# Expert stage of a hybrid decoder step: half of one weight split on GpSimd two experts ahead, tanh ahead of y's copies, gated rows turned in pieces of 128 and 384 columns

## What is computed

```
g_sel = argmax(softmax(x @ rg_w + rg_b))              # 1 of 4 groups
top_v, top_i = top_k(e_logits of that group, 2)       # 2 of its 8 experts
def expert_block(xb, e):                              # xb: 128 rows of one expert
    return (silu(xb @ w1[e]) * (xb @ w3[e])) @ w2[e]  # 1024 -> 512 -> 1024
y = sum over a token's two experts of weight * its row
```

## Time and profile before

| | |
|---|---|
| median of 3 runs | 2290.57 us (2289.27 to 2293.32) |
| profiled execution | 2292.72 us, span 2291.2 us |
| busy: TensorE, weight loads | 95%, 78% of the span |
| busy: VectorE, ScalarE, GpSimd | 65%, 43%, 18% |
| granted TensorE clock, mean | 0.974 |

### The profile page before, as it was taken

One profiled execution on the slowest core, in us unless ns is written; L12 is line 12 of the kernel. 1 busy time (PEld: TensorE's weight loads), 2 busy tenths in 40 slices (PEclk: granted clock), 3 DMA queues, 4 the chain that ended last, 5 costly groups with the idle time before them and its releaser, 6 DMA issues. The chain is left out here.

```text
span 2291.2 us, 34192 instructions
## 1 busy us (share of the span) xinstructions
PE 2184.5 (95%) x10675; PEld 1796.3 (78%) x10676; DVE 1485.8 (65%) x2864; ACT 975.2 (43%) x1569; POOL 412.0 (18%) x564
## 2 busy tenths in 40 slices
PE   6999999999899999994889999999999999989998
PEld 5888888888688888883668887888888878857775
DVE  4787777777656666554635466686666666955564
ACT  4433333334332222221535355575555555723332
POOL 1021101110234333232100000000000000033332
PEclk9999999999899999996999999999999999999999
DMA  7111101111634433322895668697775778944431
GB/s 227 58 39 65 63 33 64 64 63 70 223 102 110 145 126 134 106 79 92 304 367 190 251 217 332 250 397 290 287 276 199 289 290 324 341 153 145 156 132 54
DMA packets 160332, 407.13 MB, mean 178 GB/s; under 512 B 18835, under 2 KB 22347, under 8 KB 160014
## 3 DMA queue, kind: packets, MB, share of 16 engines
q1 hardware_dynamic: 138518, 337.17, 41.3%
q0 software_dynamic: 14560, 43.11, 5.6%
q10 hardware_dynamic: 7200, 26.22, 2.8%
HBM read 330.12 MB, written 84.82 MB: 181 GB/s over the span
## 5 line engine op out<-in xcount | busy, mean ns | idle before, releaser
L234 PE MATMUL bank<-w_hi,mix_x 128*128 128x512 f32 x816 | 338.9, 415 | 9.8 <-DMA mix_x<-xT_dram 4.3
L236 PE MATMUL bank<-w_hi,mix_x 128*128 128x512 f32 x816 | 329.0, 403 | 0.0
L235 PE MATMUL bank<-w_lo,mix_x 128*128 128x512 f32 x816 | 328.2, 402 | 0.0
L2175 DVE TENSOR_TENSOR w_lo<-raw,w_hi 128x2048 fp32r<-128x2048 f32 x130 | 289.5, 2286 | 35.6 <-ACT w_hi L2112 34.6
L2077 PE MATMUL bank<-w_hi,x_hi 128*128 128x512 f32 x784 | 306.3, 391 | 4.3 <-DVE w_lo L2175 2.2
L2079 PE MATMUL bank<-w_hi,x_lo 128*128 128x512 f32 x784 | 306.2, 391 | 0.0
L2078 PE MATMUL bank<-w_lo,x_hi 128*128 128x512 f32 x784 | 306.0, 390 | 0.0
L2112 ACT ACTIVATE w_hi<-raw 128x2048 fp32r<-128x2048 f32 x130 | 239.0, 1932 | 5.5 <-DMA raw<-in_w 5.5
L234 PEld LDWEIGHTS bank<-w_hi,mix_x 128*128 128x128 f32 x816 | 159.8, 196 | 43.2 <-issue 5.1
L236 PEld LDWEIGHTS bank<-w_hi,mix_x 128*128 128x128 f32 x816 | 159.6, 196 | 36.0
L235 PEld LDWEIGHTS bank<-w_lo,mix_x 128*128 128x128 f32 x816 | 160.1, 196 | 31.4
(11 more groups left out here) (315 smaller groups left out, 4101.6 us busy)
## 6 DMA issues: line engine op xcount, KB each, us to landing
raw<-in_w SPq DMA_DIRECT2D x128, 1024.0 KB, 8.3
shared<-in_w SPq DMA_DIRECT2D x64, 1024.0 KB, 11.5
y_dram<-y_sb ACTq DMA_DIRECT2D x50, 512.0 KB
xT_dram<-mix_x SPq DMA_DIRECT2D x34, 512.0 KB, 3.6
mix_x<-xT_dram SPq DMA_DIRECT2D x34, 512.0 KB, 4.5
shared<-in_w_in SPq DMA_DIRECT2D x24, 512.0 KB, 6.1
small<-in_x_prompt SPq DMA_DIRECT2D x16, 512.0 KB
xr_sb<-in_x_prompt SPq DMA_DIRECT2D x16, 512.0 KB
```

The costliest lines, as they stand in the source:

```text
L234: pe.matmul(bank[:, :], x_hi[:, k, :], wh[:, k, :], start=(k == 0), stop=False)
L235: pe.matmul(bank[:, :], x_hi[:, k, :], wl[:, k, :], start=False, stop=False)
L236: ins = pe.matmul(bank[:, :], x_lo[:, k, :], wh[:, k, :], start=False, stop=(k == KD - 1))
L2175: dve.tensor_tensor(w_lo[slot(j, m)][:, cols], raw[m][:, cols], w_hi[slot(j, m)][:, cols].bitcast(F32), ALU.subtract).then_inc(lo_ready, 1)
```

## The change

GpSimd computes the second half of the low half of w1 for expert e + 2, at the end of its turn of expert e, once ScalarE has written the high half; it counts a semaphore of its own, `w1_lo`. VectorE leaves that piece out (it still makes it for experts 0 and 1, and the same half of the gate weights that follow the last expert). Whoever waited for this piece waits for `w1_lo`; the counts of `lo_ready` are re-reckoned (`wait_lo`). GpSimd's loop over experts is unrolled by four. ScalarE computes tanh ahead of `y_out`. The gated rows are made, turned and copied in pieces of 128 and 384 columns; TensorE turns half of the next rows, then the first piece, then the other half, then the second piece, and y's products go by k over both column halves.

```diff
+                def wait_lo(eng, e, m, c):
+                    if m == 0 and c == 1:
+                        eng.wait_ge(w1_lo, e + 1)
+                    else:
+                        eng.wait_ge(lo_ready, 5 * e + (1, 2 + c, 4 + c)[m])
 # SyncE, reload(e)
-                                    sp_.wait_ge(lo_ready, 2 * parts_before(e - 1, m) + c + 1)
+                                    wait_lo(sp_, e - 1, m, c)
 # GpSimd
+                        def split_w1(e, j):
+                            cols = slice(RH, 2 * RH)
+                            hold(pool, hi_ready, 2 * parts_before(e, 0) + 2)
+                            pool.tensor_tensor(w_lo[slot(j, 0)][:, cols], raw[0][:, cols], w_hi[slot(j, 0)][:, cols].bitcast(F32),
+                                               ALU.subtract).then_inc(w1_lo, 1)
                         def expert(e, j):
                             first, end = span(pool, e)
                             with pool.Fori(first, end) as i:
...
                                 load_list(...)
                                 gather(i + 1)
+                            if not isinstance(e, int) or e + 2 < NE:
+                                split_w1(e + 2, j + 2)
 # TensorE
-                            transposes(i + 1)
                             for n in range(2):
+                                transposes(i + 1, n)          # four of the eight; xe_tp after n = 1
                                 pe.wait_ge(hid_ready, 2 * i + n + 1)
-                                for k in range(2 * n, 2 * n + 2):
+                                for k in range(*K_OF[n]):     # K_OF = ((0, 1), (1, 4))
...
+                            for part, ks in enumerate(K_OF):
+                                pe.wait_ge(hidT_hi_ready, 2 * i + part + 1)
+                                for k in range(*ks):
+                                    for w in (wh, wl):
+                                        for n in range(2):
+                                            pe.matmul(Y[n][:, :], hidT_hi[:, k, :], col(w, k, n), ...)
+                            pe.wait_ge(hidT_lo_ready, 2 * i + 2)
+                            for n, done in enumerate((y0_mm, y1_mm)):
+                                for k in range(KF):
+                                    ins = pe.matmul(Y[n][:, :], hidT_lo[:, k, :], col(wh, k, n), ...)
+                                ins.then_inc(done, 1)
 # ScalarE, block_of
-                            y_out(i)
                             act.wait_ge(h1_mm, i + 1)
                             act.activation(tanh_h[:, :], H1[:, :], ACT.Tanh, scale=0.5).then_inc(tanh_done, 1)
+                            y_out(i)
 # VectorE, after
+                                theirs = part[1:] == (j + 2, 0) and not (isinstance(e, int) and e + 2 == NE)
+                                split(*part, halves=(0,) if theirs else (0, 1))
```

More of the change, by code:

```diff
@@ L1903, in program @@
             lo_ready = sem("lo_ready")
+            w1_lo = sem("w1_lo")
             late_loaded = sem("late_loaded")
@@ L1928, in program @@
                 quarter = lambda bank: bank[:, :].rearrange("p (k n) -> p k n", k=4)
-                pair_of = lambda bank: quarter(bank)[:, 0:2, :]
+                K_OF = ((0, 1), (1, KF))
+                parts_of = lambda bank, n: quarter(bank)[:, 0:K_OF[n][1] - K_OF[n][0], :]
                 (xe_tp, xe_hi_ready, xe_lo_ready, h1_mm, h3_mm, tanh_done, up_done, hid_ready,
@@ L2017, in _ @@
                             for c in range(2):
-                                sp_.wait_ge(lo_ready, 2 * parts_before(NE - 1, n) + c + 1)
+                                wait_lo(sp_, NE - 1, n, c)
                                 sp_.dma_start(raw[n][:, c * RH:(c + 1) * RH].rearrange("p (k n) -> p k n", k=KD // 2),
@@ L2021, in _ @@
                                               ).then_inc(raw_loaded[n][c], 16)
-                        sp_.wait_ge(lo_ready, 2 * parts_before(NE, 0) + 2)
+                        wait_lo(sp_, NE, 0, 0)
+                        wait_lo(sp_, NE, 0, 1)
                         sp_.dma_start(w_ple, a["w_ple"][0].rearrange("(k p) n -> p k n", p=P)).then_inc(late_loaded, 16)
@@ L2041, in gather, with expert @@
                             hold(pool, rows_loaded, 16 * i + 16)
-                        def expert(e):
+                        def split_w1(e, j):
[3 more added lines that the diff above has]
+                                               ALU.subtract).then_inc(w1_lo, 1)
+                        def expert(e, j):
                             first, end = span(pool, e)
@@ L2049, in expert @@
                                 at = e * CAP + (i + 1 - first) * P
-                                if isinstance(e, int):
+                                if isinstance(e, int) and e == NE - 1:
                                     load_list(at - turned * P)
@@ L2056, in expert, with transposes @@
                                 gather(i + 1)
+                            if not isinstance(e, int) or e + 2 < NE:
+                                split_w1(e + 2, j + 2)
                         gather(0)
-                        with pool.Fori(0, NE - 1) as e:
-                            expert(e)
-                        expert(NE - 1)
+                        with pool.Fori(0, NE // SLOTS - 1) as quad:
+                            for j in range(SLOTS):
+                                expert(quad * SLOTS + j, j)
+                        for j in range(SLOTS):
+                            expert(NE - SLOTS + j, j)
                     @block.tensor
                     def _(pe):
-                        def transposes(i):
+                        def transposes(i, n):
                             pe.wait_ge(rows_loaded, 16 * i + 16)
-                            for k in range(KD):
-                                ins = pe.transpose(T[k // 4][:, (k % 4) * P:(k % 4 + 1) * P], rows_in[:, k * P:(k + 1) * P], ident[:, :])
-                            ins.then_inc(xe_tp, 1)
+                            for k in range(4 * n, 4 * n + 4):
+                                ins = pe.transpose(T[n][:, (k % 4) * P:(k % 4 + 1) * P], rows_in[:, k * P:(k + 1) * P], ident[:, :])
+                            if n:
+                                ins.then_inc(xe_tp, 1)
                         def block_of(i, e, j, first):
@@ L2073, in block_of @@
                             for m, (bank, done) in enumerate(((H1, h1_mm), (H3, h3_mm))):
-                                pe.wait_ge(lo_ready, 2 * parts_before(e, m) + 2)
+                                for c in range(2):
+                                    wait_lo(pe, e, m, c)
                                 wh, wl = w_up(w_hi, j, m), w_up(w_lo, j, m)
@@ L2086, in block_of @@
                                 ins.then_inc(hid_tp, 1)
-                            pe.wait_ge(lo_ready, 2 * parts_before(e, 2) + 2)
+                            wait_lo(pe, e, 2, 1)
                             pe.wait_ge(y_in, 2 * i + 2)
                             wh, wl = w_down(w_hi, j), w_down(w_lo, j)
+                            col = lambda w, k, n: w[:, k, n * 512:(n + 1) * 512]
+                            for part, ks in enumerate(K_OF):
[3 more added lines that the diff above has]
+                                        for n in range(2):
+                                            pe.matmul(Y[n][:, :], hidT_hi[:, k, :], col(w, k, n), start=(k == 0 and w is wh), stop=False)
@@ L2090, in block_of @@
+                            pe.wait_ge(hidT_lo_ready, 2 * i + 2)
                             for n, done in enumerate((y0_mm, y1_mm)):
-                                cols = slice(n * 512, (n + 1) * 512)
                                 for k in range(KF):
[L2093 to L2100, removed]
+                                    ins = pe.matmul(Y[n][:, :], hidT_lo[:, k, :], col(wh, k, n), start=False, stop=(k == KF - 1))
                                 ins.then_inc(done, 1)
@@ L2105, in _ @@
                         pe.sem_inc(y1_mm, 1)
-                        transposes(0)
+                        for n in range(2):
+                            transposes(0, n)
                         all_blocks(pe, block_of, None)
@@ L2135, in block_of @@
                         def block_of(i, e, j, first):
-                            y_out(i)
                             act.wait_ge(h1_mm, i + 1)
                             act.activation(tanh_h[:, :], H1[:, :], ACT.Tanh, scale=0.5).then_inc(tanh_done, 1)
+                            y_out(i)
                             for n in range(2):
                                 act.wait_ge(hid_tp, 2 * i + n + 1)
-                                copy(hidT_hi[:, 2 * n:2 * n + 2, :], pair_of(AT[n])).then_inc(hidT_hi_ready, 1)
+                                copy(hidT_hi[:, slice(*K_OF[n]), :], parts_of(AT[n], n)).then_inc(hidT_hi_ready, 1)
                             x_halves(i + 1)
@@ L2175, in split @@
```

(14 more changed lines are left out.)

2 lines of the change are left out of this document (1 added, 1 removed).

## The result

The changed kernel takes 2704.2 us in the median of 4 runs (2703.36 to 2709.37), the kernel before 2292.0 beside it: a ratio of 1.1806, 95% interval 1.1791 to 1.1821. The forecast was 2700, the range 2590 to 2820.

What follows compares the result with a forecast made beforehand. It took TensorE as the bound, busy 197.20 of 200 us in the expert stage. Thirty experts at 14.3 us more gave +428, less 6 and 10, so +412 on 2290.6: forecast 2700 us, range 2590 to 2820.

Steps and rivals of the forecast that it cites:

- The place of the wait: GpSimd's queue: the next gather stands behind its wait for ScalarE's sixth high half, 13.94 us after the row transposes.
- The count and the sum: Expert stage: 30 experts, each period 32.6 us in place of 18.38, so 14.3 us more each, 428 us.
- The -10 us for late weights: First experts: the 7.6 us wait on late weights is swallowed by the new wait, 10 us off the sum.
- The split at 4.8 us: GpSimd's 128x2048 split: 4.8 us, between 3.8 and 5.9; 4 to 6 us was named as a sign of being right.
- Rival 3: GpSimd's split slowed by VectorE's fifth split beside it: 6.9 us, total 2763; chance 0.10.
- To the list, 3.0 us: GpSimd after its split: loop end and bounds reading before the list fetch, 0 to 3.9 us, taken as 3.0.
- Rival 2: Short overheads: bounds read under the split, quiet queues with list 2.2 and gather 4.2 us; total 2563; chance 0.14.
- The low clock, 1.4 us: TensorE's transposes after some 14 us idle run at a lower clock: 1.4 us more on the chain, 0 to 1.6.
- Rival 4: TensorE's clock stays low through the y products, so ScalarE waits 2.9 us: total 2787; chance 0.10.
- Gain 12.6/48 = 0.26 us a block: 128/384 pieces remove TensorE's wait for high halves; 0.3 us for each of 19 other blocks, 6 us off the sum.
- tanh: ScalarE's tanh ahead of y's eviction: up to 0.3 us where VectorE was late, nothing while TensorE stands; cost none.
- VectorE's freed 2.2 us: VectorE makes one split less, 2.24 us for each of 30 experts, 67 us; worth nothing in the delayed periods.

Runs made afterwards that it cites:

- experiment 1: The changed kernel without the GpSimd split, VectorE making all halves, tanh first and 128/384 pieces kept: 2297.2 us, ratio 1.0020 to the kernel before.
- experiment 5: The changed kernel with GpSimd splitting w1 of e + 1 instead of e + 2 at the end of its turn of e: 2281.5 us, 0.9954.
- experiment 8: The changed kernel with GpSimd waiting at the same place but splitting nothing, VectorE making all halves: 2682.4 us, ratio 1.1696 to the kernel before.
- experiment 10: The changed kernel with VectorE making only 64 columns of w1's first half, the piece beside GpSimd's split: 2684.1 us, 1.1706.
- experiment 6: The kernel with GpSimd's split one turn later, but tanh behind y's copies and pieces of 256 columns: 2291.7 us, 0.9994.
- experiment 7: The kernel before with only the GpSimd split of the change, tanh and pieces as before: 2707.5 us, ratio 1.1805.
- experiment 2: The kernel before with nothing but tanh moved ahead of y's copies: 2292.2 us, ratio 0.9995.

## Why the prediction was right, and where it was not

*The place of the wait*: right, and shown by experiments 1, 5 and 8. The step that decided was to list what is queued on GpSimd behind its new wait and who waits for that, although the engine was 18% busy.

*The count and the sum*: right, 30 delayed gathers; 412/30 = 13.7 us each against 14.3. That 2700 met 2704 is luck in part. With the split's measured time and the 3.0 us behind it left in, the same sum gives 30 x 1.6 = 48 us more. The -10 us for late weights came true at the two periods that they lengthen (22.3 and 27.4 us before, 20.5 and 20.3 after: -8.9), but the first delayed gather took 15.3 us to land, and its period 44.9 us instead of 20.3. And the sum is a chain of durations and says nothing on what each is worth. Removing the split's 6.35 us wins 22 us (experiment 8), not 190: bounds are read and weights pass beneath it.

*The split at 4.8 us*: its own time is 4.59, and 1.76 is waiting for VectorE; 6.35 is outside the 4 to 6 us named as a sign. Rival 3 had the mechanism (6.9 us), held for loosely borne out; its 2763 did not come, since the term behind the split went the other way. The Trainium skill, "GPSIMD Engine Reference", section "Performance versus the Vector engine", gives 4497 ns for 2048 fp32 columns; the 4594 ns measured are 2% above it. The Trainium skill, on the same page, section "Specifications", names contention with VectorE instructions that have two SBUF inputs; experiment 10 agrees, with 4.59 us without VectorE's split beside it and 6.35 us with it.

*To the list, 3.0 us*: nothing, the low end of the 0 to 3.9; 3.2 where no split covers it. Rival 2 had this half of its case right, but not the quiet queues: list and gather took 4.9 and 4.3 us, not 2.2 and 4.2.

*The low clock, 1.4 us*: 1.2 on the chain of a single-block expert. In a two-block expert it is paid in the first period instead, which lies wholly on the path, and there it costs 0.9 to 2.1 us, while the late period is about 1 us shorter for starting at full clock. So its price is moved more than raised: some 0.6 us more for such an expert, which the sum left out. Rival 4, the clock low through all of y, did not happen. The transposes began at 1505.80; the clock was 0.50 in the 5 us around that and 0.93 in the next 5:

```profile
1505.00:1510.00 5.00, 4.20 (x16) 3.92 (x17) 1.11 (x3) 1.62 (x5) 0.00 (x0) 0.50 0.01 5
1510.00:1515.00 5.00, 5.00 (x22) 4.02 (x22) 4.00 (x4) 5.00 (x4) 0.00 (x0) 0.93 0.00 0
```

*"Gain 12.6/48 = 0.26 us a block" for the pieces*: wrong by itself. I priced the wait they remove and not what is late next in the 32 of 49 blocks after splits, although show `up` starting as the sixth split ends. Alone they lose 4 us; with VectorE relieved they are, with tanh's move, worth 10 us (experiment 5 against 6). In the change it did not show, since they act there on undelayed blocks alone, and the 6 us that the sum took off for them are not seen either (experiment 7).

*tanh*: right, nothing (experiment 2). *VectorE's freed 2.2 us*: right that it is worth nothing while TensorE stands; with the split one turn later it is one of the two conditions of the gain of 11 us.

## What to carry to other kernels

An idle engine that fetches is not free: before work with a wait is given to it, write down what stands behind that wait in its queue, and place the wait where the thing awaited is made before the next fetch is due; here one turn later, with the same other edits, turned +412 us into -11. And when two limits lie within a few tenths of a microsecond, single edits read as nothing or as a small loss: measure them together before dropping either.

## What the runs showed of the hardware

The splits of GpSimd and of VectorE, each an operation with two SBUF inputs, do not run side by side: in the overlaps shown here one waits until the other has ended. When GpSimd came first by 0.3 us, in the first split of the changed kernel, VectorE's took 6.68 us instead of 2.28, about the 4.5 more that GpSimd still needed, and GpSimd's 4.81:

```profile
1139.95 4.81 POOL L2058 TENSOR_TENSOR w_lo<-shared,w_hi 128x2048 fp32r<-128x2048 f32 x1 [26.95 <-ACT w_hi L2137]
...
1140.23 6.68 DVE L2200 TENSOR_TENSOR w_lo<-shared,w_hi 128x2048 fp32r<-128x2048 f32 x1
```
```profile
1520.77 2.28 DVE L2200 TENSOR_TENSOR w_lo<-shared,w_hi 128x2048 fp32r<-128x2048 f32 x1
1522.97 0.68 DVE L2205 SCALAR_TENSOR_TENSOR up<-tanh_h,bank 128x512 f32<-128x512 f32 x1
```

When VectorE came first (1520.77 to 1523.05, with GpSimd from 1521.12), GpSimd took 6.36 us, 1.8 more than alone, about the 1.9 that VectorE still needed. `up`, with one input in PSUM, ran its usual 0.68 us during GpSimd's split. And GpSimd read its next bounds while its split computed: the list was issued 0.05 us before the split's end (1527.43 and 1527.48), but 3.2 us after the wait where there was no split.
